# Identity products into an unread PSUM bank while TensorE waits, in a two-block transformer kernel

## The reference

```python
def first_block(...):                      # DEPTH = 2 layers
    for l in range(DEPTH):
        ...                                # nine modulation rows: cond @ w_ada[l] + b_ada[l]
        y = _swiglu(_modulate(x, sh1, sc1), ffn1_w_gate[l], ffn1_w_up[l], ffn1_w_down[l])
        x = _post_norm(x, y, g1, FFN_RES, ln_gain[l, 0], ln_bias[l, 0])
        y = _token_mixer(_modulate(x, sh2, sc2), w_in[l], w_out[l])   # three kinds of attention
        x = _post_norm(x, y, g2, 1.0, ln_gain[l, 1], ln_bias[l, 1])
        y = _swiglu(_modulate(x, sh3, sc3), ffn2_w_gate[l], ffn2_w_up[l], ffn2_w_down[l])
        x = _post_norm(x, y, g3, FFN_RES, ln_gain[l, 2], ln_bias[l, 2])

def second_block(...):                     # DEPTH = 2: attention and pooling, then a convolution
    for layer in range(DEPTH):
        ...
        h_lat = _post_norm_2(h_lat, m_lat[2] * y_lat, ...)
        f_lat = _expert_choice_ffn(_modulate_2(h_lat, m_lat[3], m_lat[4]), w_router[layer], ...)
        h_lat = _post_norm_2(h_lat, m_lat[5] * f_lat, ...)

def _expert_choice_ffn(u, w_router, w_g, w_u, w_d):    # 16 experts, each takes 32 of 256 tokens
    logits = jnp.einsum('bnd,de->ben', u, w_router)
    aff = jax.nn.softmax(logits, axis=1)
    gate, idx = lax.top_k(aff, cap)
    ...
```

## Time and profile before

| | us |
|---|---|
| median of 3 runs | 2454.43 (2452.34 to 2455.11) |
| the profiled execution's own time | 2456.58 |
| its span in the profile | 2454.4 |
| PE busy | 2068.7 (84%) |
| DVE busy | 1149.8 (47%) |
| ACT busy | 553.8 (23%) |
| PE's idle time until DVE's `x_tok` (L1717), 12 times | 50.2 |

### The profile page before, as it was taken

One profiled execution on the slowest core, in us unless ns is written; L12 is line 12 of the kernel. 1 busy time (PEld: TensorE's weight loads), 2 busy tenths in 40 slices (PEclk: granted clock), 3 DMA queues, 4 the chain that ended last, 5 costly groups with the idle time before them and its releaser, 6 DMA issues.

```text
span 2454.4 us, 33654 instructions
## 1 busy us (share of the span) xinstructions
PE 2068.7 (84%) x12564; PEld 1317.7 (54%) x12564; DVE 1149.8 (47%) x1755; ACT 553.8 (23%) x885; POOL 65.6 (3%) x96
## 2 busy tenths in 40 slices
PE   5998997999899898899997877777769787777775
PEld 4998454998799545699874422222229442222221
DVE  3887676878787775777643210000026421000002
ACT  3333133333433223333332100000023110000000
POOL 0000000000000000000200000000000000000000
PEclk8999998999899898999998877777769888777777
DMA  8986775889588685688843899999996679999996
GB/s 328 334 297 252 272 247 180 282 293 330 194 289 292 233 287 185 233 307 308 271 160 146 306 409 410 410 410 410 410 385 221 244 307 410 410 410 409 410 410 258
DMA packets 290910, 758.08 MB, mean 309 GB/s; under 512 B 17616, under 2 KB 127472, under 8 KB 290720
## 3 DMA queue, kind: packets, MB, share of 16 engines
q1 hardware_dynamic: 283904, 737.34, 80.3%
q0 software_dynamic: 6688, 19.78, 2.4%
q10 hardware_dynamic: 256, 0.13, 0.0%
HBM read 756.01 MB, written 1.18 MB: 309 GB/s over the span
## 4 chain that ended last, share of the span: by engine, by line
PE 57%; DMA 21%; SPq 11%; DVE 5%; ACT 2%; issue 2%; DVEq 1%; ACTq 0%
PE psum L804 21%; DMA W<-in_w_exp_up 16%; PE psum L816 10%; SPq L547 10%; PE psum L844 5%; PE psum L867 4%; PE psum L1152 3%; PE psum L1243 3%; DMA W_mod<-in_mod_w 3%; DMA W<-in_w_exp_down 2%; PE psum L1045 1%; PE psum L1183 1%; PE psum L1166 1%; PE psum L773 1%; PE psum L1198 1%
## 5 line engine op out<-in xcount | busy, mean ns | idle before, releaser
L804 PE MATMUL psum<-parts 128*128 128x256 f32 x4224 | 527.9, 285 | 13.3 <-DVE parts L1657 7.3
L804 PEld LDWEIGHTS psum<-parts 128*128 128x128 f32 x4224 | 525.4, 194 | 20.7 <-issue 14.4
L1152 PE MATMUL psum<-W,scr 128*32 128x512 f32 x1936 | 287.2, 702 | 139.1 <-DMA W<-in_w_exp_up 135.2
L2126 DVE TENSOR_TENSOR scr<-scr,psum 128x256 f32<-128x256 f32 x32 | 13.5, 421 | 563.9 <-ACT scr L1528 563.9
L1608 DVE SCALAR_TENSOR_TENSOR mod_acc<-W_mod,cond,mod_acc 128x1024 f32<-128x1024 f32 x196 | 251.8, 1285 | 51.8 <-issue 27.8
L816 PE MATMUL psum<-parts 128*128 128x512 f32 x1056 | 257.8, 393 | 0.0
L1152 PEld LDWEIGHTS psum<-W,scr 128*32 128x32 f32 x1936 | 49.8, 115 | 349.0 <-DMA W<-in_w_exp_up 270.0
L1737 DVE TENSOR_TENSOR parts<-W,parts 128x1024 fp32r<-128x1024 f32 x176 | 207.2, 1219 | 57.4 <-ACT parts L1320 57.4
L1183 PE MATMUL psum<-W,scr 128*32 128x256 f32 x2048 | 187.1, 523 | 38.7 <-DMA W<-in_w_exp_down 22.5
L816 PEld LDWEIGHTS psum<-parts 128*128 128x128 f32 x1056 | 192.6, 188 | 45.3 <-DVE parts L1750 8.2
L1320 ACT ACTIVATE parts<-W 128x1024 fp32r<-128x1024 f32 x176 | 175.9, 1051 | 69.2 <-issue 46.4
(11 more groups left out here) (299 smaller groups left out, 1690.6 us busy)
## 6 DMA issues: line engine op xcount, KB each, us to landing
W<-in_w_exp_down SPq DMA_DIRECT2D x128, 1024.0 KB
W_mod<-in_mod_w SPq DMA_DIRECT2D x123, 1024.0 KB, 5.3
W<-in_w_exp_gate SPq DMA_DIRECT2D x242, 512.0 KB, 14.7
W<-in_w_exp_up SPq DMA_DIRECT2D x242, 512.0 KB, 15.7
W<-in_ffn_w_gate SPq DMA_DIRECT2D x44, 1024.0 KB, 8.4
W<-in_ffn_w_up SPq DMA_DIRECT2D x44, 1024.0 KB, 10.8
W<-in_ffn_w_down SPq DMA_DIRECT2D x44, 1024.0 KB, 9.5
W<-in_w_in SPq DMA_DIRECT2D x24, 1024.0 KB, 8.5
```

The source lines that it names most:

```text
L804: ins = pe.matmul(psum[:, 4 + t % 2, S * g:S * g + S], w[:, t % 2, g, kc, :], u[:, kc, :], start=(n == 0 and kc == 0), stop=(n == 2 and kc ...
L1152: ins = pe.matmul(psum[32 * q:32 * q + 32, 4, :].rearrange("p (g n) -> p g n", g=2), xe_now[:, b, :], w[:, :, q, :], start=(b == 0), stop= ...
```

## The change

A helper `keep_running(bank, n)` issues n products: the stationary operand is the 128x128 identity, the moving one the tile of ones, 128x128, read twice (256 columns), both float32, the result goes to 256 columns of one bank. No wait and no signal is attached to them in the code. They stand at 36 places, 243 products in all: opening 23; the five seams of the first block that follow a feed-forward or mixer, 104; the two mixers 34; both routers 52; the seam ahead of the convolution 24; ahead of its last product 6. Nothing else is changed.

```diff
--- before.py
+++ after.py
@@ -726,6 +726,12 @@
         def _(pe):
             ident = K["ident"]
 
+            def keep_running(bank, n):
+
+                for _ in range(n):
+                    pe.matmul(psum[:, bank, 0:256], ident[:, :], K["ones"][:, :].unsqueeze(1).to_broadcast([P, 2, P]),
+                              start=True, stop=True, skip_group_check=True)
+
             def mod_quarter(job, done, c, bank=6, first=None):
 
                 if c == 0:
@@ -774,10 +780,14 @@
                     if kc % 4 == 3:
                         ins.then_inc(tr_pe, 1)
 
-            def turn_tiles(first):
+            def turn_tiles(first, waits=None):
 
                 for t in range(TT):
+                    if waits:
+                        keep_running(0 if t else 7, waits[t])
                     turn_tile(first + t, t)
+                if waits:
+                    keep_running(0, waits[2])
 
             def turned_first(inst, kc):
                 if kc % 2 == 0:
@@ -958,6 +968,7 @@
                 pe.wait_ge(m_act.s, m_act.at("qk4", l))
                 pe.wait_ge(m_dve.s, m_dve.at("qk5", l))
                 scores(1)
+                keep_running(2, 6)
                 second(0)
                 pe.wait_ge(m_act.s, m_act.at("ev00", l))
                 project(1, 0, 0)
@@ -984,6 +995,7 @@
                 pe.wait_ge(m_dve.s, m_dve.at("qk1", l))
                 scores(4)
                 pe.wait_ge(m_dve.s, m_dve.at("y1", l))
+                keep_running(3, 3)
                 values(3)
                 scores(5)
                 pe.wait_ge(m_act.s, m_act.at("ev20", l))
@@ -991,6 +1003,7 @@
                 values(4)
                 values(5)
                 project(2, 1, 4)
+                keep_running(7, 8)
                 turn(y_tok, lambda t: (m_dve.s, m_dve.at("y", l)))
                 turned(l * 4 + 2)
                 times_rows(uT, lambda u: slot(MIX_IN_USES + u), lambda: row_sum(4)).then_inc(m_pe.sig("out"), 1)
@@ -1000,6 +1013,9 @@
                     if 4 * job + c == 6:
                         pe.wait_ge(s_const, 16 * (len(CONSTS) - len(MIXER_ONLY)))
                         turn_tiles(1)
+                        keep_running(3, 9)
+                    if 4 * job + c == 7:
+                        keep_running(3, 2)
                     mod_quarter(job, job, c, bank=job, first=job)
             for job in range(FIRST_JOBS):
                 pe.wait_ge(mod_taken, job + 1)
@@ -1007,15 +1023,16 @@
                     ins = pe.matmul(psum[:, 2, 8 * job + h:8 * job + 8:2], first_row[job][:, P * h:P * h + P], ident[:, 0:97:32],
                                     start=True, stop=True)
             ins.then_inc(pe_cols, 1)
+            keep_running(3, 12)
             for l in range(LAYERS):
                 if l:
-                    turn_tiles(6 * l + 1)
+                    turn_tiles(6 * l + 1, (15, 8, 5))
                 turned(l * 4)
                 ffn(l, 0)
-                turn_tiles(6 * l + 3)
+                turn_tiles(6 * l + 3, (11, 8, 3))
                 turned(l * 4 + 1)
                 mixer(l)
-                turn_tiles(6 * l + 5)
+                turn_tiles(6 * l + 5, (0, 11, 5))
                 turned(l * 4 + 3)
                 ffn(l, 1)
 
@@ -1111,8 +1128,11 @@
             def experts(layer):
 
                 for t in range(TT):
+                    if t:
+                        keep_running(1, 4)
                     turn_tile(15 + 4 * layer + t, t)
                     if t:
+                        keep_running(1, 3)
                         turned(10 + 2 * layer)
                     for kc in range(KC):
                         if t == 0:
@@ -1120,15 +1140,18 @@
                         ins = pe.matmul(psum[:, 0, EXPERTS * t:EXPERTS * t + EXPERTS], uT[:, kc, P * t:P * t + P],
                                         part(w_router[:, layer, :], 0, KC, EXPERTS)[:, kc, :], start=(kc == 0), stop=(kc == KC - 1))
                 ins.then_inc(r_pe.sig("logits"), 1)
+                keep_running(1, 4)
                 pe.wait_ge(r_dve.s, r_dve.at("aff", layer))
                 for t in range(TT):
                     ins = pe.transpose(psum[0:EXPERTS, 5, P * t:P * t + P], routeT[:, t, EXPERTS:2 * EXPERTS], ident[:, :])
                 ins.then_inc(r_pe.sig("affT"), 1)
+                keep_running(1, 13)
                 pe.wait_ge(r_dve.s, r_dve.at("slot", layer))
                 for t in range(TT):
                     ins = pe.transpose(psum[:, 5, EXPERTS * t:EXPERTS * t + EXPERTS], route[0:EXPERTS, 3, P * t:P * t + P],
                                        ident[0:EXPERTS, 0:EXPERTS])
                 ins.then_inc(r_pe.sig("slotT"), 1)
+                keep_running(1, 2)
                 pe.wait_ge(r_dve.s, r_dve.at("sel", layer))
                 for kc in range(KC):
                     for t in range(TT):
@@ -1222,7 +1245,7 @@
             experts(0)
 
 
-            turn_tiles(17)
+            turn_tiles(17, (11, 8, 5))
             turned(11)
             for fb in range(KC):
                 if fb >= 2:
@@ -1245,6 +1268,7 @@
                     if (n, p) == (0, 2):
                         ins.then_inc(cv_pe.sig(f"f{fb}a"), 1)
                 ins.then_inc(cv_pe.sig(f"f{fb}"), 1)
+            keep_running(0, 6)
             pe.wait_ge(cv_dve.s, cv_dve.at("f7"))
             times_rows(conv_yT, lambda u: in_slot("cout", u)).then_inc(cv_pe.sig("out"), 1)
             experts(1)
```

## The result

| | before | after |
|---|---|---|
| median of 4 runs each, us | 2453.44 (2452.34 to 2455.11) | 2415.93 (2413.52 to 2417.11) |
| the profiled execution's own time, us | 2456.58 | 2417.11 |
| its span, us | 2454.4 | 2414.9 |
| mean granted TensorE clock | 0.873 | 0.924 |

What follows compares the result with a forecast made beforehand. Outside the experts TensorE's products, cut by norm waits and then half-clocked, were the chain; in the experts, HBM's weight stream. Gains of 8.4 + 12.5 + 2.2 + 5.1 + 0.9 = 29.1, less 0.5 and 1.5, gave 27: about 2427 us, range 2412 to 2442.

Steps and rivals of the forecast that it cites:

- the second step: Everywhere: one new product costs 0.215 us at full clock, 0.425 at half; 243 are 52 or 103 us.
- slower: Rival: new products outlast their waits, deciding price 0.6 us each; at 0.7 about 2477 us; chance 0.04.
- What of it the new products bring: Step comparing idle time left in each wait with 2.1 us, after which the clock was down; gains sum to 29.1.
- stage starts: Split-operand and mixer starts after seams: mostly full clock, 0.8 of 7.8 + 3.2, 8.8 us; new low-part wait about 0.3.
- the mixers' last wait: Behind the mixers' last wait: 4.4 less eight products leaves 2.7, over 2.1, so half of 4.5, 2.2 us.
- the short waits: Waits in both mixers and before the convolution's last product: idle left at or under 2.1, so all 8.4 us.
- the routers: Both routers: thirteen products leave 3.5 of the 6.3 wait, thin load after; three tenths of 17.0, 5.1 us.
- VectorE's slack: Mixers' first products: VectorE idled 1.80 us for them, so gain capped near 1.8 per mixer, 3.2 of 5.5 us.
- The overruns: Products outlasting their waits at half clock, as the router's four (1.7 in 1.65): 0.5 us over all places.
- Clock falls all the same: Rival: seams, routers and opening keep half clock, only short waits gain, about 2446 us; chance 0.16 together with slack.
- slack: Rival: VectorE and DMAs pace the mixers' first half, perhaps feed-forwards; gain some 16, 2440 us; chance 0.16 with clock falls.
- Nothing: Rival: unread products of constant tiles may not hold the clock, so nothing moves, 2454 us; chance 0.05.

Runs made afterwards that it cites:

- the seams' kernel: Changed kernel with new products kept only in the first block's seams and ahead of the convolution (128 products): 2440.1 us, ratio 0.9938.
- the routers' kernel: Changed kernel with new products kept only in the two routers (52 products): 2439.77 us, ratio 0.9944.

## Why the prediction was right in sign and short in size

**The price of one new product failed**, the second step: "Two of them take 0.43 us at full clock and 0.85 at half, so 0.215 and 0.425 each". The rows were right and their reading was wrong. L893 x2 are not two products but the two instructions of one float32 product; it costs 0.43 and 0.85 us. This could have been seen before: in the code the logits (L1120) are eight products for each tile, and the trace has sixteen instructions for them, as after at L1140 x16; the transposes have eight for eight. The Trainium skill ("FP8 and Floating Point Precision", TensorE Precision Notes) says that true float32 makes four passes through the array: an estimate from it, 4 times 256 columns at 2.4 GHz, is 0.43 us for a product, and the trace agrees with 0.43. A price that is read from a row has to be divided by what the code wrote, not by the row's count.

**Here luck helped.** The prediction held that the number "fits even at half clock". With the price read right it does not: eleven products are 9.4 us in a wait of 5.33, and all 243 are 207 us in waits of some 120. Its rival "slower" set the deciding price at 0.6 us for each, which the true half-clock price of 0.85 passes, so it deserved more than 4 in 100. That nothing was lost came from the clock, which was up when most of the new products ran, so that they ended inside nearly all their waits (0.48, 0.34 and 0.32 us left over in the first seam).

**What followed from it.** The new work is 115.1 us busy, not 52. In the terms of "What of it the new products bring" the idle time left in a seam was not 3.0 us but 0.5, and in the router's long wait not 3.5 but 0.64. The fractions, eight tenths for stage starts, half for transposes and the last wait, three tenths for routers, were chosen for half-filled waits that the kernel did not have.

**How much that mattered, the kernel with half the products says.** It has about the work that the prediction reckoned with, and gained 28.6 us where 27 were worked out. Its terms agree by place, apart from the mixers' last wait (3.9 against 2.2). In the seams it won 13.7 and the full number 14.5, at the short waits 8.3 and 8.4; only in the routers 4.6 and 10.1. So the halved price put one term wrong, the routers. The others were short by less, the seams by 2.0, the mixers' last wait by 1.7, the opening by 0.9; and 2 us had been taken off for overruns and held starts, which the measured terms already contain.

**The short waits** were 8.4 in the forecast and 8.4 by the table, but 3.2 of it, behind `values(3)`, was also won by two kernels that fill nothing there. The prediction took a fall of the clock in one execution for one that comes each time; that this term came out right is luck in part.

**The routers** were the mis-sized term, 5.1 forecast, 10.1 measured. Half a filling gave 4.6, the full one 10.1 here and 15.0 and 15.2 in two other kernels; in the changed kernel, of the ceiling of 17.0 what is missing is the two overruns of 1.6, and the first expert's blocks in both routers at 0.50 (3.4 us each in the windows after, 1.8 us each at 0.52 per microsecond).

**The mixers' last wait** gave 3.9 instead of 2.2: with 3.62 us of products in the wait of 4.4, it leaves 0.91 and the clock stays up. With half it was 3.9 as well, so here the step "leaves 2.7, over 2.1: half" was wrong by itself: behind the 2.64 us that the kernel with half the products left idle there in layer 0, the clock was at 1.00. Here too some is chance: in layer 1 the seams' kernel, with no product at this wait, won 1.3 of the 2.6.

**VectorE's slack** was taken right in kind, and the cap was wrong in form. The forecast capped what a mixer's first products win at some 1.8 us. With their transposes they won 3.8 and 4.4, and gave back 2.1 and 2.6 until L904's place; what stayed is 1.7 and 1.8. This agreement with the cap is in part chance: by the same matching the other kernels with filled seams kept between 0.5 and 3.0 us per mixer. The rotation that had waited 1.80 us starts without a wait, 4.62 us earlier. The timeline of VectorE after shows where it is lost:

```profile
263.33 0.69 DVE L1820 TENSOR_TENSOR gate_att<-scr,k_mixer 128x512 f32<-128x512 f32 x1
...
287.52 0.75 DVE L1630 TENSOR_SCALAR mod_acc<-W_mod,cond 128x1024 f32<-128x1024 f32 x1 [6.46 <-DMA W_mod<-in_mod_w]
```

By 287.52 it is only 3.81 earlier (291.33 before, where this wait for a chunk was 5.58): the chunks' stream gives less than TensorE does. Then TensorE waits 2.91 us for that row, where it had waited 1.54, and behind this longer wait its clock is down, which takes another 0.75:

```profile
301.28 0.77 PE L758 MATMUL psum<-mod_acc,k_ones 128*32 128x256 f32 x8 [2.91 <-DVE mod_out L1646]
301.98 1.97 PE L890 MATMUL psum<-k_ident,scr 128*128 128x128 f32 x8
```

The eight transposes took 1.20 before. So behind a wait that the change has lengthened the clock can come down at a new place. It does not always: in layer 1 of the same execution the same wait was 3.21 us, and the transposes behind it took 1.20.

**The overruns** were 0.5 in the forecast, and are 3.2, all at the four products ahead of the second tile in the routers. The prediction had named this place (1.7 in 1.65) and a doubled price at half clock makes it 3.4 in 1.65. With the same four products two other kernels lost 1.0 and 0.8 in all.

**The stage starts** held as told: the 96 products of the opening take 11.75 us, and 80 of the 96 at the second feed-forward's start 9.85, from the chain of waits; the low part of the operands (`u_lo`) has become a wait. Sixteen products at 0.123 are 1.97 and the seventeenth starts 2.25 after the first, so it is 0.28, forecast 0.3.

```profile
43.76 11.75 PE psum L814 x96
...
412.45 1.23 DVE parts L1689
...
413.72 9.85 PE psum L814 x80
```

**The rivals.** "Clock falls all the same" and "slack" were for less; both had the mechanism of the half-filled seam in mind, which did not come. "Nothing" is refuted. "Slower" had set its deciding price at 0.6 us for each product; the kernel with twice the number puts 0.86 of full-clock work in place of each 0.43 and is 38.4 us slower than before, so the point lies between the two; no run places it closer.

**Open.** The second block's attention lost 0.9 us, and its last product won 1.5; both go with the clock falling or not falling at places that the change doesn't touch, as in the routers' kernel, and may be the chance of one execution. Of the 29 us of doubled products that vanished, 13 are not placed. Why the clock falls behind the same wait in one execution and not in another is not shown.

## What to carry to other kernels

Where an engine's clock follows its load, a wait costs twice, and filling it with work that no one reads takes back the second part: here 37.5 us. Size the filling by time, read at full clock and counted per product of the code: half of each wait already gave three quarters of the gain, the full wait the rest, twice the wait lost it all and as much again. Look first whether what follows the wait is paced by TensorE at all, and count what is left in the waits behind it: a stage that is won earlier can meet a stream that comes no faster, and its longer wait can bring the clock down at a new place. Do not price a place by one trace in which the clock falls behind a short wait: look whether it falls there in a second one.

## What was not expected of the hardware

- A float32 product of 256 columns stands in the trace as two instructions of 0.216 us at full clock, a transpose of 128 columns of the same type as one of about 0.11 (44 in 4.96 us, with the tail of the last).
- Transposes alone, with nothing else in the waits, kept the granted clock at 1.00 in the three windows looked at (2411.82 us, ratio 0.9832, 0.9815 to 0.9848).
- The clock fell without any long wait, too: at 1308.6 in the router (0.50 from there to 1312.0), where TensorE had done sixteen instructions of 16 columns behind a wait of 0.52 us, and at 1332.5 behind products of 64 columns and a wait of 1.54 us.
- The clock does not always fall behind the same work. In the kernel with two products ahead of the router's second tile the first expert's blocks took 7.07 us in the first router and 8.77 in the second, behind the same wait of 1.54 us. Nine executions of the kernel before had mean granted clocks from 0.871 to 0.911, and times from 2451.57 to 2458.64 us.
